# Padding a rank-one bias in attention scores from 64 to 128 partitions, in a two-layer decoder trunk

## The chip, the cores and the metric

The program runs on one core of a Trainium2 chip. The time is the device time of one execution in microseconds, and lower is better. A kernel's time is the median of several executions; the profile and the trace come from one execution of their own.

## The reference

The trunk has two layers over x of 256 tokens by 2048 channels, all in float32. Layer 0 mixes tokens by attention with a forget gate, layer 1 by a short gated convolution; each mixer is followed by an MLP of width 8192. Every sub-layer is normalised (RMSNorm), shifted and scaled by a vector worked out from c, and added back through a gate. The part that matters here is the attention of layer 0, with 16 heads of 128 channels:

```python
def fox_attention(q, k, v, log_f):
    F = jnp.cumsum(log_f.astype(jnp.float32), axis=-1)
    def one_block(args):                                    # 128 queries
        blk, q_i, F_i = args
        s = jnp.einsum('bhqd,bhkd->bhqk', q_i, k).astype(jnp.float32) * scale
        s = s + F_i[..., :, None] - F[..., None, :]
        q_pos = blk * Q_BLOCK + jnp.arange(Q_BLOCK)
        s = jnp.where(k_pos[None, :] <= q_pos[:, None], s, -jnp.inf)
        p = jax.nn.softmax(s, axis=-1)
        return jnp.einsum('bhqk,bhkd->bhqd', p.astype(v.dtype), v)
```

log_f is the log sigmoid of 16 forget logits per token, so F has one row of 256 values for each head. The term -F[s] is the same for all queries of a head.

## The kernel before

**Weights.** All products run on TensorE (PE) in a split form: every float32 operand becomes a high part (rounded by ACT) and a low part (the remainder, by DVE), and each product is three matmuls, high by high, low by high, high by low. Weights stream from memory through `raw` (four quarters of a unit of 2048 rows by 512 columns, issued by SP, queue `raw_arrived`). ACT writes `w_hi` (L790), DVE writes `w_lo` (L1183), both in a ring of four slots, each slot a pair of 128-row chunks. A unit has eight pairs. A slot is freed when PE has used it (`split_used`), and a quarter of `raw` when DVE has split it, so that SP then asks for the same quarter of the next unit. `chan_pair` (L428 to L430) makes q and k with channels on partitions, 24 matmuls of 256 columns a pair; `tok_pair` (L441 to L443) makes v and the outputs with tokens on partitions, 12 matmuls of 512 columns a pair.

**Beside it** POOL issues loads of the conditioning weights (`ada_raw`, four tiles), and DVE accumulates them (L1195, L1198) between its splits; the steps per slot are written out in tables. PE sums the result with ones (`ada_sum`).

**Attention.** Four groups of four heads. In the stream of each group PE calls `scores(g)` after an early pair of a unit (the pair of index 2 of unit 3 for group 0, index 1 of the v unit for the others), `turn_probs(g)` after its last pair, and `mix_values(g)` after the pair of index 2 of the next q unit (one unit later for group 0). Between them DVE takes the maxima (L1404, L1406), ACT the exponentials (L949), DVE normalises (L1421).

**`scores`** is the only reader of the two tiles of the change. For each of four heads and two query blocks it issues five matmuls into one group: three for q times k (L637 to L639), one that adds -F (L640), one that adds the causal mask (L641, weights `ident_r`). For query block 0 the first four cover 128 keys, for block 1 they cover 256; L641 covers 128. L640 is the special one: its weights are one column of `sel`, repeated 128 times, and it multiplies the tile `nf`.

**`nf` and `sel`.** `log_f` holds 64 columns: the 16 heads at columns 0 to 15 and again at 32 to 47, with zeros between and behind. A matmul with a triangle of ones (`upto`, L577) turns them into 64 rows of sums in PSUM. ACT copies them negated into `nf` [64, 256] (L914, rounded), and DVE puts the remainder into rows 32 to 47 (L1330). Column h of `sel` [64, 16] has ones in row h and row 32 + h, so that the matmul over 64 partitions picks the high and the low part of head h and adds them. Both tiles are filled or prepared by POOL at the start: memsets (L382 to L388), then the selections (L391 to L402), each raising `const_ready`. PE waits on it before its first transposition (L500, of the conditioning vector c by `ident`) and before the sums (L575), DVE before it copies the gates (L1322).

Of the kernel before, what the change touches and what calls it, by code (L numbers as in the profile page):

```python
# [5 lines left out]
F32 = mybir.dt.float32  # L6
F32R = mybir.dt.float32r
ACT = mybir.ActivationFunctionType
# [3 lines left out]
P = 128  # L12
D = 2048
T = 256
H = 16
# [10 lines left out]
NB = NU // P  # L26
# [76 lines left out]
def build(nc, x, c, ada_w, ada_b, norm_mix, norm_mlp, fox_w_in, fox_b_f, fox_w_out,  # L103
          conv_w_in, conv_w, conv_w_out, mlp_w_up, mlp_w_down, final_norm, out):
    ctx = ExitStack()
    with ctx:
        def sb(name, shape, dt=F32):
            return ctx.enter_context(nc.sbuf_tensor(name, shape, dt))

        def sem(name):  # L110
            return ctx.enter_context(nc.semaphore(name))

        def over(tensors):
# [6 lines left out]
            ("start_ring", [P, RING, 2, 2, NU], F32), ("xnT", [P, KC, T], F32), ("vrow", [VROWS, 4, P], F32),  # L120
            ("upto", [P, TT, T], F32), ("wf", [P, KC, H], F32), ("wf_hi", [P, KC, H], F32R), ("wf_lo", [P, KC, H], F32R)])
        _, conv_b, conv_c, _, gate = over([
            ("at_qs", [P, 2, QK, NU], F32), ("conv_b", [P, NB, T], F32), ("conv_c", [P, TT, NU], F32),
            ("to_vs", [P, QK, NU], F32), ("gate", [P, D], F32)])
# [6 lines left out]

        final_row, y = over([("final_row", [P, D], F32), ("y", [P, TT, D], F32)])
        _, square_out = over([("at_h", [P, 2 * (KC - 2) * T], F32), ("square_out", [P, 2 * NU], F32)])
        h = sb("h", [P, KC, 2, T], F32R)
        hb = sb("hb", [P, 2, EK, T])
# [24 lines left out]
        ident_r = sb("ident_r", [P, P], F32R)  # L160
        causal = sb("causal", [P, P], F32R)
        ones = sb("ones", [P, P])
        sel = sb("sel", [4 * H, H], F32R)
        vcol = sb("vcol", [P, 4, VROWS])
        c_col = sb("c_col", [P, KC])
        ca = sb("ca", [P, KC])
# [2 lines left out]
        gain = sb("gain", [P, KC])  # L169
        bf = sb("bf", [H, 1])  # L170
        log_f = sb("log_f", [P, TT, 4 * H])
        nf = sb("nf", [4 * H, T], F32R)
        f_tok = sb("f_tok", [P, TT, H])
        row_max = sb("row_max", [P, TT, NB])
        exp_bias = sb("exp_bias", [P, TT, NB])
# [10 lines left out]
        ps = ctx.enter_context(nc.psum_tensor("ps", [P, 8, NU], F32))  # L186
# [17 lines left out]
        const_ready = sem("const_ready")  # L204
# [34 lines left out]
        f_act = sem("f_act")  # L239
# [67 lines left out]
        def ada_tile(i, k):  # L307
            b, n = ADA[i]
            layer, part = PARTS[b]
            return ada_w[layer][P * k:P * (k + 1), D * part + NA * n:D * part + NA * (n + 1)]  # L310
# [69 lines left out]
        @block.gpsimd  # L380
        def _(pool):
            pool.memset(ident[:, :], 0.0).then_inc(const_ready, 1)  # L382
            pool.memset(ident_r[:, :].bitcast(F32), 0.0).then_inc(const_ready, 1)
            pool.memset(causal[:, :].bitcast(F32), 0.0).then_inc(const_ready, 1)
            pool.memset(upto[:, :, :], 1.0).then_inc(const_ready, 1)
            pool.memset(ones[:, :], 1.0).then_inc(const_ready, 1)
            pool.memset(sel[:, :].bitcast(F32), 0.0).then_inc(const_ready, 1)
            pool.memset(log_f[:, :, :], 0.0).then_inc(const_ready, 1)  # L388
            pool.wait_ge(const_ready, 7)
            for m in (ident, ident_r):  # L390
                pool.affine_select(out=m[:, :], in_=m[:, :].bitcast(F32), compare_op=ALU.not_equal, fill=1.0,  # L391
                                   base=0, pattern=[[-1, P]], channel_multiplier=1).then_inc(const_ready, 1)

            for i in range(2):
                pool.wait_ge(const_ready, 9 + i)
                pool.affine_select(out=sel[:, :], in_=sel[:, :].bitcast(F32), compare_op=ALU.not_equal, fill=1.0,
                                   base=-2 * H * i, pattern=[[-1, H]], channel_multiplier=1).then_inc(const_ready, 1)
            pool.affine_select(out=causal[:, :], in_=causal[:, :].bitcast(F32), compare_op=ALU.is_ge, fill=MASKED,
                               base=0, pattern=[[-1, P]], channel_multiplier=1).then_inc(const_ready, 1)
            for a in range(TT):  # L400
                pool.affine_select(out=upto[:, a, :], in_=upto[:, a, :], compare_op=ALU.is_ge, fill=0.0,
                                   base=-P * a, pattern=[[1, T]], channel_multiplier=-1).then_inc(const_ready, 1)  # L402

            for t in range(KC * A_END):
                if t < TILES:
                    pool.wait_ge(start_steps, START_STEPS[START_TILES - 1 + t // 2])
                    if t >= 2:
                        pool.wait_ge(start_used, START_TILES // 2)
                else:
                    pool.wait_ge(ada_steps, t - TILES + 1)  # L410
                pool.dma_start(ada_raw[:, t % TILES, :], ada_tile(t // KC, t % KC)).then_inc(ada_arrived[t % TILES], 16)  # L411

        @block.tensor
        def _(pe):
# [82 lines left out]
                return hooks  # L497


            pe.wait_ge(const_ready, 8)  # L500
            pe.wait_ge(c_arrived, 16)
            turn(ps[:, 4, 0:KC], vrow[0:KC, 0, :], ident[0:KC, 0:KC]).then_inc(c_turned, 1)
            pe.wait_ge(c_step, 4)
# [68 lines left out]

            def forget_sums():
                pe.wait_ge(f_step, 5)
                pe.wait_ge(const_ready, 14)  # L575
                for a in range(TT):
                    mm(ps[0:4 * H, 7, 0:T], log_f[:, a, :], upto[:, a, :], start=(a == 0), stop=(a == TT - 1))  # L577
                for b in range(TT):
                    for a in range(TT):
                        last = mm(ps[:, 7, T + H * b:T + H * (b + 1)], upto[:, a, P * b:P * (b + 1)], log_f[:, a, 0:H],  # L580
                                  start=(a == 0), stop=(a == TT - 1))
                last.then_inc(f_done, 1)
# [30 lines left out]
            for i in range(6):  # L613
                start_pair(n + i)
                if i == 2:
                    forget_turn()
                if i == 4:
                    forget_sums()
# [5 lines left out]
            def scores(g):  # L624
                pe.wait_ge(evacuated[(3 * g) % 2], (3 * g) // 2 + 1)
                pe.wait_ge(evacuated[(3 * g + 1) % 2], (3 * g + 1) // 2 + 1)
                pe.wait_ge(attn_ready, g)
                if g == 0:
                    pe.wait_ge(evacuated[0], 2)
                    pe.wait_ge(f_rows, 2)  # L630
                q = qs if g else mid[:, NB:2 * NB, :, :]
                for j in range(NB):
                    pick = sel[:, NB * g + j:NB * g + j + 1].broadcast_to([4 * H, P])
                    for b, o in ((0, ps[:, 6, P * j:P * (j + 1)]), (1, ps[:, 4 + j // 2, T * (j % 2):T * (j % 2 + 1)])):
                        n = P * (b + 1)
                        qh, ql = q[:, j, 0, P * b:P * (b + 1)], q[:, j, 1, P * b:P * (b + 1)]
                        mm(o, qh, ks[:, j, 0, 0:n], start=True, stop=False)  # L637
                        mm(o, qh, ks[:, j, 1, 0:n], start=False, stop=False)
                        mm(o, ql, ks[:, j, 0, 0:n], start=False, stop=False)  # L639
                        mm(o, pick, nf[:, 0:n], start=False, stop=False)  # L640
                        last = mm(o[:, n - P:n], ident_r[:, :], causal[:, :], start=False, stop=True)  # L641
                last.then_inc(scores_done, 1)
# [26 lines left out]
            for u in range(3, 3 * NG):  # L669
                g, t = u // 3, u % 3  # L670
# [87 lines left out]
            for i in range(3 * NG):  # L758
                g, t = i // 3, i % 3
# [21 lines left out]
        def _(act):  # L781
            op = nc.scalar.activation
# [128 lines left out]

            def forget_rows():
                act.wait_ge(f_done, 3)
                op(nf[:, :], ps[0:4 * H, 7, 0:T], ACT.Copy, scale=-1.0).then_inc(f_act, 1)  # L914

            def round_start(i):

# [20 lines left out]
            start_split(n + 8)  # L938
            start_split(n + 9)
            forget_rows()  # L940
            round_start(2)

# [30 lines left out]
            for u in range(3, 3 * NG):  # L973
                g, t = u // 3, u % 3
# [170 lines left out]
            for i in range(3 * NG):  # L1145
                g, t = i // 3, i % 3
# [29 lines left out]
        def _(dve):  # L1176
# [142 lines left out]

            def forget_copy():  # L1320
                dve.wait_ge(f_done, 2)
                dve.wait_ge(const_ready, 14)  # L1322
                for c0 in (0, 2 * H):
                    v.tensor_copy(log_f[:, :, c0:c0 + H], ps[:, 6, 64:64 + TT * H].rearrange("p (a h) -> p a h", a=TT)
                                  ).then_inc(f_step, 1)
# [61 lines left out]
            forget_log()  # L1387
            start_split(n + 4)
            forget_copy()
            start_split(n + 5)  # L1390
            low_start(0)
# [80 lines left out]
            for u in range(3, 3 * NG):  # L1472
                g, t = u // 3, u % 3
# [218 lines left out]
            for i in range(3 * NG):  # L1692
                g, t = i // 3, i % 3
# [40 lines left out]
```

## Time and profile before

| | us |
|---|---|
| median of three executions | 2396.4 |
| the three | 2382.73, 2396.4, 2397.29 |
| profiled execution, its own time | 2394.39 |
| its span, first to last instruction | 2392.7 |
| granted clock of TensorE over the span | 0.979 |

| engine | busy us | share of the span |
|---|---|---|
| PE matmuls | 2320.2 | 97% |
| PE weight loads | 1952.3 | 82% |
| DVE | 1630.4 | 68% |
| ACT | 1052.2 | 44% |
| POOL | 173.1 | 7% |

Matmuls overlap in the records: the duration of one is its latency, and the pace of the stream is read from the distance of the starts. PEld stands for the weight loads, which may run ahead of their matmul. The granted clock is a share of 2.4 GHz, so 0.50 is 1.2 GHz. The stage of q, k, v and attention lies between about 130 and 450 us; the output projection, MLP, convolution and second MLP follow. Calls of `scores` start at 164.52, 221.80, 310.56 and 395.95 us.

### The profile page before, as it was taken

What the parts mean: (1) busy time and instruction counts of PE and PEld (TensorE: products, weight loads), DVE (VectorE), ACT (ScalarE), POOL (GpSimd) and SP (SyncE); (2) the same over time, 40 slices, a digit from 0 to 9 for tenths busy, and PEclk for the clock granted to TensorE, in tenths of its full rate; (3) what the DMA queues carried; (4) which work ended last, traced back from release to release, by engine and by line L of the source; (5) the groups of instructions that cost most, each with busy time, mean ns of one, the idle gap of its engine ahead of it and who ended that gap; (6) DMA issues with size and microseconds to landing.
All of it is one profiled execution on the core that took longest, in us unless ns stands there. A gap on an engine that the chain in (4) does not pass through costs nothing.

```text
span 2392.7 us, 29047 instructions
## 1 busy us (share of the span) xinstructions
PE 2320.2 (97%) x11331; PEld 1952.3 (82%) x11331; DVE 1630.4 (68%) x1539; ACT 1052.2 (44%) x1183; POOL 173.1 (7%) x338
## 2 busy tenths in 40 slices
PE   5999999989999999999998999998999999999998
PEld 5988989768888888888886888876888888888886
DVE  5757877767866766776776888755786455455455
ACT  4344433445434434434444444444543443443443
POOL 0001111100100100100100111100010000000000
PEclk8999999999999999999998999999999999999999
DMA  9978878767977977987984899854896655655563
GB/s 364 387 247 282 310 275 334 269 245 246 313 274 246 314 277 239 323 281 227 324 282 161 312 339 332 310 164 153 280 320 208 194 189 185 191 192 190 190 201 122
DMA packets 270530, 615.61 MB, mean 257 GB/s; under 512 B 14704, under 2 KB 15040, under 8 KB 269504
## 3 DMA queue, kind: packets, MB, share of 16 engines
q1 hardware_dynamic: 220480, 437.29, 53.9%
q0 software_dynamic: 46080, 167.79, 19.7%
q10 hardware_dynamic: 3840, 8.68, 1.0%
q8 instruction: 95, 1.56, 0.3%
q14 instruction: 35, 0.29, 0.0%
HBM read 611.62 MB, written 2.10 MB: 257 GB/s over the span
## 4 chain that ended last, share of the span: by engine, by line
PE 90%; DMA 3%; DVE 3%; ACT 2%; issue 1%; SPq 0%; ACTq 0%; DVEq 0%
PE ps L441 26%; PE ps L443 26%; PE ps L442 26%; DMA start_ring<-in_ada_w_dram 3%; PE ps L428 2%; PE ps L430 2%; PE ps L429 2%; PE ps L720 1%; PE ps L481 1%; PE ps L478 1%; ACT w_hi L790 1%; DVE acc L1198 1%; DVE w_lo L1183 1%; PE ps L640 0%; PE ps L641 0%
## 5 line engine op out<-in xcount | busy, mean ns | idle before, releaser
L1183 DVE TENSOR_TENSOR w_lo<-raw,w_hi 128x1024 fp32r<-128x1024 f32 x740 | 903.8, 1224 | 624.8 <-ACT w_hi L790 622.5
L790 ACT ACTIVATE w_hi<-raw 128x1024 fp32r<-128x1024 f32 x740 | 783.6, 1060 | 1149.1 <-PE ps L443 1060.7
L441 PE MATMUL ps<-w_hi,h 128*128 128x512 f32 x1536 | 610.1, 397 | 6.5 <-DVE h L1296 6.5
L443 PE MATMUL ps<-w_lo,h 128*128 128x512 f32 x1536 | 602.6, 392 | 0.0
L442 PE MATMUL ps<-w_hi,h 128*128 128x512 f32 x1536 | 602.2, 392 | 0.0
L441 PE MATMUL ps<-w_hi,mid 128*128 128x512 f32 x1280 | 503.7, 393 | 2.6 <-DVE mid L1689 2.6
L443 PE MATMUL ps<-w_lo,mid 128*128 128x512 f32 x1280 | 499.6, 390 | 0.0
L442 PE MATMUL ps<-w_hi,mid 128*128 128x512 f32 x1280 | 499.2, 390 | 0.0
L441 PEld LDWEIGHTS ps<-w_hi,h 128*128 128x128 f32 x1536 | 291.4, 190 | 69.0 <-issue 9.3
L443 PEld LDWEIGHTS ps<-w_lo,h 128*128 128x128 f32 x1536 | 291.0, 189 | 62.1
L442 PEld LDWEIGHTS ps<-w_hi,h 128*128 128x128 f32 x1536 | 291.7, 190 | 59.2 <-issue 0.5
L411 POOL DMA_DIRECT2D ada_raw<-in_ada_w_dram x320 | 169.7, 531 | 1621.2 <-DVE acc L1195 571.0
L441 PEld LDWEIGHTS ps<-w_hi,mid 128*128 128x128 f32 x1280 | 241.1, 188 | 53.9 <-issue 4.5
L442 PEld LDWEIGHTS ps<-w_hi,mid 128*128 128x128 f32 x1280 | 241.2, 188 | 50.8 <-issue 1.4
L443 PEld LDWEIGHTS ps<-w_lo,mid 128*128 128x128 f32 x1280 | 240.9, 188 | 50.9
L1198 DVE SCALAR_TENSOR_TENSOR acc<-ada_raw,ca,acc 128x1024 f32<-128x1024 f32 x150 | 191.9, 1280 | 1.7 <-DMA ada_raw<-in_ada_w_dram 0.8
L1198 DVE SCALAR_TENSOR_TENSOR hb<-ada_raw,ca,hb 128x1024 f32<-128x1024 f32 x150 | 191.9, 1279 | 1.5 <-DMA ada_raw<-in_ada_w_dram 1.0
L428 PE MATMUL ps<-h,w_hi 128*128 128x256 f32 x512 | 149.0, 291 | 0.0
L430 PE MATMUL ps<-h,w_lo 128*128 128x256 f32 x512 | 147.3, 288 | 0.0
L429 PE MATMUL ps<-h,w_hi 128*128 128x256 f32 x512 | 147.3, 288 | 0.0
L428 PEld LDWEIGHTS ps<-h,w_hi 128*128 128x128 f32 x512 | 100.9, 197 | 0.2
L429 PEld LDWEIGHTS ps<-h,w_hi 128*128 128x128 f32 x512 | 101.1, 197 | 0.0
(201 smaller groups left out, 1248.6 us busy)
## 6 DMA issues: line engine op xcount, KB each, us to landing
ada_raw<-in_ada_w_dram POOLq DMA_DIRECT2D x320, 512.0 KB, 6.3
raw<-in_mlp_w_up_dram SPq DMA_DIRECT2D x128, 1024.0 KB, 5.3
raw<-in_mlp_w_down_dram SPq DMA_DIRECT2D x128, 1024.0 KB, 6.4
raw<-in_fox_w_in_dram SPq DMA_DIRECT2D x48, 1024.0 KB, 9.2
raw<-in_conv_w_in_dram SPq DMA_DIRECT2D x48, 1024.0 KB, 7.2
start_ring<-in_ada_w_dram SPq DMA_DIRECT2D x64, 512.0 KB, 11.7
raw<-in_fox_w_out_dram SPq DMA_DIRECT2D x16, 1024.0 KB, 7.7
raw<-in_conv_w_out_dram SPq DMA_DIRECT2D x16, 1024.0 KB, 5.2
```

The source lines that it names most:

```text
L411: pool.dma_start(ada_raw[:, t % TILES, :], ada_tile(t // KC, t % KC)).then_inc(ada_arrived[t % TILES], 16)
L428: mm(o, hi[:, jc], xh, start=(k == 0 and j % 2 == 0), stop=False, skip_group_check=True)
L429: mm(o, hi[:, jc], xl, start=False, stop=False, skip_group_check=True)
L430: last = mm(o, lo[:, jc], xh, start=False, stop=(k == KC - 1), skip_group_check=True)
L441: mm(o, xh, hi, start=(k == 0), stop=False)
L442: mm(o, xl, hi, start=False, stop=False)
L443: last = mm(o, xh, lo, start=False, stop=(k == KC - 1))
L478: last = mm(ps[:, SUM - 1 + b, :], ones[:, :], accs[slot][:, NU * b:NU * (b + 1)], start=True, stop=True)
L481: last = mm(ps[:, SUM, j:j + 1], accs[slot][:, P * j:P * (j + 1)], ones[:, 0:1], start=True, stop=True)
L790: op(w_hi[:, e % WR], raw[:, e // 2, EK * (e % 2):EK * (e % 2 + 1)], ACT.Copy).then_inc(hi_ready, 1)
L1183: v.tensor_tensor(w_lo[:, e % WR], raw[:, e // 2, EK * (e % 2):EK * (e % 2 + 1)], w_hi[:, e % WR].bitcast(F32), ALU.subtract).then_inc(spl ...
L1198: v.scalar_tensor_tensor(slot, src, ca[:, col:col + 1], slot, ALU.mult, ALU.add).then_inc(steps, 1)
```

## The change

`sel` and `nf` get 128 partitions. POOL sets all of `nf` to zero at the start, one instruction more, and all counts of `const_ready` rise by one. The partitions 64 to 127 of both stay zero; ACT and DVE write the same rows as before. L640 contracts over 128 partitions, and ACT waits for POOL before it writes `nf`.

```diff
@@ -160,7 +160,7 @@
-        sel = sb("sel", [4 * H, H], F32R)
+        sel = sb("sel", [P, H], F32R)
@@ -169,7 +169,7 @@
-        nf = sb("nf", [4 * H, T], F32R)
+        nf = sb("nf", [P, T], F32R)
@@ -386,13 +386,14 @@
             pool.memset(log_f[:, :, :], 0.0).then_inc(const_ready, 1)
-            pool.wait_ge(const_ready, 7)
+            pool.memset(nf[:, :].bitcast(F32), 0.0).then_inc(const_ready, 1)
+            pool.wait_ge(const_ready, 8)
...
-                pool.wait_ge(const_ready, 9 + i)
+                pool.wait_ge(const_ready, 10 + i)
@@ -497,7 +498,7 @@
-            pe.wait_ge(const_ready, 8)
+            pe.wait_ge(const_ready, 9)
             pe.wait_ge(c_arrived, 16)
@@ -572,7 +573,7 @@
             def forget_sums():
                 pe.wait_ge(f_step, 5)
-                pe.wait_ge(const_ready, 14)
+                pe.wait_ge(const_ready, 15)
@@ -630,7 +631,7 @@
                 for j in range(NB):
-                    pick = sel[:, NB * g + j:NB * g + j + 1].broadcast_to([4 * H, P])
+                    pick = sel[:, NB * g + j:NB * g + j + 1].broadcast_to([P, P])
@@ -911,7 +912,8 @@
             def forget_rows():
                 act.wait_ge(f_done, 3)
-                op(nf[:, :], ps[0:4 * H, 7, 0:T], ACT.Copy, scale=-1.0).then_inc(f_act, 1)
+                act.wait_ge(const_ready, 15)
+                op(nf[0:4 * H, :], ps[0:4 * H, 7, 0:T], ACT.Copy, scale=-1.0).then_inc(f_act, 1)
@@ -1319,7 +1321,7 @@
                 dve.wait_ge(f_done, 2)
-                dve.wait_ge(const_ready, 14)
+                dve.wait_ge(const_ready, 15)
```

The one place where an instruction is added is on POOL, ahead of the identity that PE's first transposition needs. POOL's order from the memset of `sel` on, in the kernel before:

```order
L387 MEMSET sel 64x16
L388 MEMSET log_f 128x128
L391 ISA
L391 AFFINE_SELECT ident<-ident 128x128
L391 AFFINE_SELECT ident_r<-ident_r 128x128
```

and in the changed kernel, whose lines behind the memset are one higher:

```order
L387 MEMSET sel 128x16
L388 MEMSET log_f 128x128
L389 MEMSET nf 128x256
L392 ISA
L392 AFFINE_SELECT ident<-ident 128x128
L392 AFFINE_SELECT ident_r<-ident_r 128x128
```

The memset of `nf` now stands between that of `log_f` and the two selections that make the identities, and everything behind it on POOL comes one memset later. On PE, DVE and ACT the instructions and their order are the same as before.

## Rows read from the trace of the kernel before

**Rows 1.** The page, part 1: busy us, share of the span, instructions.

```profile
PE 2320.2 (97%) x11331; PEld 1952.3 (82%) x11331; DVE 1630.4 (68%) x1539; ACT 1052.2 (44%) x1183; POOL 173.1 (7%) x338
```

**Rows 2.** Waits of PE, 130 to 420 us: total us, times, longest.

```profile
PE ps L648 <- DVE scratch L1421: 2.7, 2, 1.4
```

**Rows 3.** Line 640: count, ns min/median/max, first and last start, forms.

```profile
L640 PE MATMUL ps<-nf,sel x32: 322/382/579, 164.9 to 404.8; 64*128 64x128 f32 x16, 64*128 64x256 f32 x16
```

**Rows 4.** Timeline of PE, one head in `scores`: start us, us, what.

```profile
166.29 0.28 PE L637 MATMUL ps<-ks,mid 128*128 128x128 f32 x1
...
166.51 0.27 PE L639 MATMUL ps<-ks,mid 128*128 128x128 f32 x1
166.72 0.32 PE L640 MATMUL ps<-nf,sel 64*128 64x128 f32 x1
166.97 0.33 PE L641 MATMUL ps<-causal,ident_r 128*128 128x128 f32 x1
167.13 0.33 PE L637 MATMUL ps<-ks,mid 128*128 128x256 f32 x1
...
168.10 0.28 PE L637 MATMUL ps<-ks,mid 128*128 128x128 f32 x1
```

**Rows 5.** Timeline of PE, first of `mix_values(0)` and the matmul behind its last.

```profile
199.19 0.28 PE L661 MATMUL ps<-mid,vs 128*128 128x256 f32 x1
...
201.90 0.34 PE L428 MATMUL ps<-h,w_hi 128*128 128x256 f32 x1
```

**Rows 6.** Timeline of the weight loads, same head as rows 4.

```profile
166.45 0.19 PEld L639 LDWEIGHTS ps<-ks,mid 128*128 128x128 f32 x1
166.72 0.18 PEld L640 LDWEIGHTS ps<-nf,sel 64*128 64x128 f32 x1
166.97 0.19 PEld L641 LDWEIGHTS ps<-causal,ident_r 128*128 128x128 f32 x1
```

**Rows 7.** Timeline of PE around the first and the second call of `scores`.

```profile
164.16 0.28 PE L428 MATMUL ps<-h,w_hi 128*128 128x256 f32 x1
...
164.52 0.22 PE L637 MATMUL ps<-ks,mid 128*128 128x128 f32 x1
...
172.17 0.52 PE L428 MATMUL ps<-h,w_hi 128*128 128x256 f32 x1
...
174.67 0.28 PE L428 MATMUL ps<-h,w_hi 128*128 128x256 f32 x1
...
221.12 0.39 PE L441 MATMUL ps<-w_hi,h 128*128 128x512 f32 x1
...
221.80 0.22 PE L637 MATMUL ps<-ks,qs 128*128 128x128 f32 x1
...
231.34 0.73 PE L441 MATMUL ps<-w_hi,h 128*128 128x512 f32 x1
...
236.26 1.84 PE L481 MATMUL ps<-ones,acc 128*128 128x1 f32 x16
```

**Rows 8.** Windows: length, PE busy (count), granted clock, DMA share, GB/s.

```profile
225.60:235.80 10.20, 10.20 (x31) 0.50 0.62 239
...
399.70:409.80 10.10, 10.10 (x30) 0.50 0.90 346
170.95:174.30 3.35, 3.35 (x15) 0.51 0.33 130
...
199.20:201.90 2.70, 2.70 (x27) 1.00 0.95 325
```

**Rows 9.** Timeline of the first 9 us: POOL's widest memset; DVE after its copy.

```profile
1.24 0.53 POOL L385 MEMSET upto<- 128x512 f32 x1
...
8.72 0.17 DVE L1260 TENSOR_SCALAR ce<-ce 128x16 f32<-128x16 f32 x1 [5.52 <-ACT ce L830]
```

**Rows 10.** DMA busy share in tenths, 40 slices of 394 to 416 us.

```profile
DMA  9999999999999999999999999841000000000008
```

**Rows 11.** Waits of DVE, 150 to 450 us: total us, times, longest.

```profile
DVE acc L1198 <- DMA ada_raw<-in_ada_w_dram: 0.8, 1, 0.8
```

## The prediction

> **What bounds the kernel now.** The page's first part comes first: PE's matmuls are busy 97% of the span [rows 1]. The waits of PE between 130 and 420 us, the stage that makes q, k and v and runs the attention, hold one line of 2.7 us [rows 2]; so in that stage PE's own stream sets the pace, and what lengthens that stream lengthens the kernel. Then PE's timeline inside `scores`, the only user of the two tiles. Line 640 runs 32 times, all of them on 64 partitions [rows 3]: four heads, two query blocks each, in four calls.
>
> In one head's ten matmuls [rows 4] the starts tell the price of the 64-row matmul. From L639 to L640 it takes 0.21 us, from L640 to L641 0.25 us and from L641 to the next L637 0.16 us. Between neighbours that both have 128 rows the step is 0.11 us (166.29 to 166.51 is two of them). The whole head takes 168.10 - 166.29 = 1.81 us. For comparison, `mix_values` issues 24 matmuls on 128 rows, half of them 128 and half 256 columns wide, in 201.90 - 199.19 = 2.71 us [rows 5], 0.113 us each, whichever the width. Ten at that pace are 1.13 us. The weight loads say why [rows 6]: the load of L639 starts at 166.45, ahead of its matmul (166.51), while the loads of L640 and L641 start at 166.72 and 166.97, the very starts of their matmuls. Around the 64-row matmul nothing is loaded in advance, on the way in and on the way out.
>
> The second thing to see is the clock. Four stretches show half of the granted clock, 1.2 in place of 2.4 GHz, one at each call of `scores` [rows 8]: 225.6 to 235.8 at the second, one of the same length at the third, 399.7 to 409.8 at the fourth (0.50 each), and 170.95 to 174.3 (0.51) at the first. Ahead of the first two the engine had issued the stalled stream of `scores` for 6.4 and 3.8 us (from 164.52 and 221.80 [rows 7]). In `mix_values`, of the same matrix sizes without the 64-row matmul, the granted clock stayed at 1.00 [rows 8].
>
> **The change part by part.** *One more memset and a longer wait on POOL.* `nf` is 128x256; the 128x512 memset of `upto` took 0.53 us [rows 9], so this one costs 0.27 to 0.53, say 0.3. It delays the identity and with it the first transposition, whose product DVE copies, and then DVE sits idle for 5.52 us until ACT's exponential [rows 9]. That idle time covers it: nothing, and 0.3 us if it were gone. The other waits on `const_ready` come up at 150 us and later, when POOL has long been done; `sel` grows in partitions only, as does what L640 reads. The wait added on ACT before `nf` is written has no one behind it for the same reason. Nothing.
>
> *The switch between 64 and 128 rows, at full clock.* Four heads at 1.81 are 7.24 us a call. Four at 1.13 are 4.52; after a 128-wide group some steps of 0.17 stand in the old rows (a 256-wide one follows), so I take 4.55. Saved: 2.69 a call, 10.8 in four.
>
> The Trainium skill ("TensorEngine Tiling (Array Packing)", Key Properties) says that changing the tiling mode drains TensorE; 64 rows of 128 is a mode of its own there, and the trace agrees with a drain in the three late steps. Against this change speaks "TensorE: Matmul & The Clock Gate" (Why this matters for your kernels): a matmul on 32 rows takes the time of one on 128, so widening by itself would give nothing. By the first the sum stands; by the second alone it would be zero. The trace bears out both, since L640's own load is no shorter or longer, and the loss is at the borders.
>
> *The clock, if it no longer falls.* Read from [rows 7], as start of `scores`, its end, and the start after the twelve matmuls that follow. First call: 172.17 - 164.52 = 7.65, then twelve of L428 to L430 in 2.50 where full clock gives 12 x 0.12 = 1.44. Second call: 231.34 - 221.80 = 9.54, then twelve of L441 to L443 in 236.26 - 231.34 = 4.92 where full clock gives 12 x 0.227 = 2.72 (three took 0.68 ahead of the call). The third and fourth repeat the second, with half clock for as long [rows 8]. Beyond 7.24 at full clock the loss is 0.41 + 1.06 = 1.47 in the first and 2.30 + 2.20 = 4.50 in each of three: 15.0 in all. I take it as won back whole, since the new stream is 4.55 us at the pace of `mix_values`, which kept its clock. The other end is that nothing of it comes back: a stream of 4.55 us is longer than the 2.71 that the trace shows unharmed.
>
> *Does the rest follow?* The queue behind `scores` on PE is the next weight pairs. ACT and DVE split weights only as PE frees slots, so in `scores` they stand idle and start again when the next pair is done: their work, the maxima, exponentials and the turn of the probabilities all hang on that pair and move ahead with it. What could be late next is the transfers. Around the fourth call the DMA engines are full until about 408 us, then idle until 415 [rows 10]; the call began at about 395.9 if the clock fell 3.8 us into it, as in the second. With the change the next pair would end at 395.9 + 4.55 + 2.72 = 403.2, some 5 us before the queue runs dry. In the whole stage only 0.8 us of DVE's time waited for a transfer [rows 11]. I count nothing for this and price it as a rival.
>
> **Sum.** 10.8 + 15.0 = 25.8 us off the profiled execution's 2394.4, so 2368.6. The median of the three runs, 2396.4, lies 2.0 above that execution; on its scale the forecast is 2370.6.
>
> **Rivals.**
> *The clock falls all the same.* It would take back the 15.0: gain 10.8, 2385.6. For it: all four calls lost it, and the new ones still run 4.55 us of narrow matmuls. Against: `mix_values` did not.
> *The gain is eaten by transfers.* The stage keeps DMA full before each of the last three calls. If every slot needed its load at once, the restart would wait for the queue: 5 us at the fourth call, by the same reading at most as much at the second and third, none at the first, up to 15; with some 12, gain 14, 2382.6. Against: the 0.8 us above, and that the raw tiles are asked for a whole unit ahead.
> *It does not do what it says.* If the late loads came from the data (one column repeated 128 times as weights) and not from the rows, the steps stay: 2396.4. Against: L641 has plain weights and is late too. The skill's rule on few rows, above, would by itself land here too.
> *Slower.* The same cause, but with twice the rows to fetch the stall doubles: 0.68 more for each of 16 heads, 10.8 more, 2407.2. It needs the load's time to grow with its rows, and decides from any growth above zero; 128-row loads take 0.19 us where L640's takes 0.18 [rows 6], so nearly nothing speaks for it.
>
> **How the numbers follow.** Forecast 0.78, clock falls 0.08, transfers 0.09, no effect 0.04, slower 0.01. The forecast's own spread comes from the other stretches of half clock in the program, which can fall longer or shorter (one like those above is worth 4.5), and from the runs of before, which lie 14.6 us apart: 2362 to 2380 (two such stretches below the forecast, two above). To hold 8 in 10 I reach up through the two partial gains to 2386. About 1% (24 us) is what a measurement can tell from no change, and the limit for faster by over 1% is 2372.4, close above the forecast; a little over six tenths of its 0.78 lie beyond it, 0.48. Within 1%: 0.51. Slower by over 1%: 0.01, since even the slower rival stays within.
>
> **What would show it.** In the changed profile L640 has 128 rows, its weight load starts ahead of its matmul, all steps are 0.11 to 0.17, a call of `scores` takes 4.5 to 4.8 us, and the granted clock is 1.00 through each call and the pair behind it. DVE's idle time at each call shrinks by as much, and q/k/v and attention end about 26 us earlier. Wrong would be: steps of 0.2 and more at L640 or L641; half clock at `scores`; new waits of PE on w_lo or of DVE on transfers between 240 and 450 us.

## The result and the profile after

The changed kernel took 2370.02 us (median of six executions, 2369.65 to 2373.3), the kernel before 2389.26 us (six, 2382.73 to 2397.29). The ratio is 0.9917, 95% interval 0.9896 to 0.9939: faster by 0.8%. The forecast was 2370.6; it had set out from a median of 2396.4, which more executions of before brought down.

The head and part 1 of the page of the changed kernel, which answer to [rows 1]:

```profile
span 2368.4 us, 29049 instructions
PE 2302.1 (97%) x11331; PEld 1944.2 (82%) x11331; DVE 1629.6 (69%) x1539; ACT 1052.0 (44%) x1183; POOL 172.6 (7%) x339
```

The span is 24.3 us shorter with the same number of matmuls. Lines behind the memset stand one higher, so L641 is the bias matmul that was L640. Its record, to be read against [rows 3]:

```profile
L641 PEld LDWEIGHTS ps<-nf,sel x32: 187/190/193, 164.9 to 381.9; 128*128 128x128 f32 x32
L641 PE MATMUL ps<-nf,sel x32: 273/278/283, 165.0 to 382.0; 128*128 128x128 f32 x16, 128*128 128x256 f32 x16
```

It has 128 rows, its median latency fell from 382 to 278 ns, and the last call is over at 382.2 us where it was at 405.5. PE's timeline in the second call, which answers to [rows 4] and [rows 7] (start us, us, what):

```profile
217.84 0.22 PE L638 MATMUL ps<-ks,qs 128*128 128x128 f32 x1
217.89 0.28 PE L639 MATMUL ps<-ks,qs 128*128 128x128 f32 x1
218.01 0.27 PE L640 MATMUL ps<-ks,qs 128*128 128x128 f32 x1
218.12 0.27 PE L641 MATMUL ps<-nf,sel 128*128 128x128 f32 x1
218.23 0.27 PE L642 MATMUL ps<-causal,ident_r 128*128 128x128 f32 x1
218.34 0.34 PE L638 MATMUL ps<-ks,qs 128*128 128x256 f32 x1
...
222.34 0.45 PE L442 MATMUL ps<-w_hi,h 128*128 128x512 f32 x1
```

All steps into and out of L641 shown here are 0.11 us (0.11 to 0.12 in the rest of the call), and the call takes 222.34 - 217.84 = 4.50 us, where it took 9.54. The weight loads are in advance again, as the loads of L641 and L642 show against [rows 6]:

```profile
166.06 0.19 PEld L641 LDWEIGHTS ps<-nf,sel 128*128 128x128 f32 x1
166.17 0.19 PEld L642 LDWEIGHTS ps<-causal,ident_r 128*128 128x128 f32 x1
```

Their matmuls start at 166.12 and 166.23. The windows of the four calls (length, PE busy, PEld, DVE, ACT, POOL, granted clock, DMA share, GB/s) show a granted clock of 1.00, where [rows 8] had 0.50:

```profile
164.70:169.20 4.50, 4.50 (x42) 4.50 (x41) 3.24 (x3) 1.06 (x1) 0.96 (x2) 1.00 0.91 314
217.90:222.30 4.40, 4.40 (x41) 4.40 (x40) 3.50 (x3) 1.06 (x1) 0.98 (x2) 1.00 0.98 350
299.50:303.90 4.40, 4.40 (x41) 4.40 (x40) 3.95 (x4) 1.06 (x1) 0.80 (x3) 1.00 1.03 397
377.70:382.10 4.40, 4.40 (x40) 4.40 (x39) 4.40 (x5) 1.06 (x1) 0.53 (x1) 1.00 1.02 391
```

### The profile page after: what moved, and what is told of

Its sections match the earlier page's. It is cut to its first block, busy times and chain, and to the rows that moved or that the text cites. A ratio compares the mean times of both kernels' runs of the same rounds, so it can differ in the third digit from the quotient of the medians.

```text
span 2368.4 us, 29049 instructions
## 1 busy us (share of the span) xinstructions
PE 2302.1 (97%) x11331; PEld 1944.2 (82%) x11331; DVE 1629.6 (69%) x1539; ACT 1052.0 (44%) x1183; POOL 172.6 (7%) x339
## 4 chain that ended last, share of the span: by engine, by line
PE 90%; DVE 3%; DMA 3%; ACT 2%; issue 1%; SPq 0%; ACTq 0%; DVEq 0%
PE ps L442 26%; PE ps L444 26%; PE ps L443 26%; DMA start_ring<-in_ada_w_dram 3%; PE ps L429 2%; PE ps L431 2%; PE ps L430 2%; PE ps L721 1%; PE ps L482 1%; PE ps L479 1%; ACT w_hi L791 1%; DVE acc L1200 1%; DVE w_lo L1185 1%; PE ps L516 1%; ACT scratch L951 0%
## 6 DMA issues: line engine op xcount, KB each, us to landing
start_ring<-in_ada_w_dram SPq DMA_DIRECT2D x64, 512.0 KB, 11.7
```

## The experiments

Each run is timed beside the kernel before on the same chip. The ratio given with its 95% interval need not be the quotient of the two medians beside it. Three questions: is it the border between row counts, or something else in the change or in the matmul; which row counts have a border; and what does the half clock hang on.

### The tiles alone

```diff
-    pick = sel[:, NB * g + j:NB * g + j + 1].broadcast_to([P, P])
+    pick = sel[0:4 * H, NB * g + j:NB * g + j + 1].broadcast_to([4 * H, P])
...
-    mm(o, pick, nf[:, 0:n], start=False, stop=False)
+    mm(o, pick, nf[0:4 * H, 0:n], start=False, stop=False)
```

> The changed kernel, with L641 reading only partitions 0 to 63 of the two larger tiles: the added memset and waits stay, the width of the matmul goes back. Theory (the borders between 64 and 128 rows cost the time): one head takes 1.81 us again, the calls 7.6 to 9.6 us, half clock of 3.4 to 10.2 us at each call, and the time is that of the kernel before, within 3 us. Rival (larger tiles or the order of the start do it): the time of the changed kernel, 2370.

Measured: 2389.04 us against 2390.32 of before, ratio 0.9999 (0.9986 to 1.0013). The profile has the stalls and the half clock back; windows of this kernel, with the same columns as above:

```profile
170.60:177.40 6.80, 6.80 (x25) 5.67 (x26) 0.00 (x0) 0.00 (x0) 0.21 (x1) 0.50 0.49 179
228.60:238.80 10.20, 10.20 (x31) 7.97 (x31) 0.04 (x1) 0.00 (x0) 0.53 (x1) 0.50 0.67 259
317.40:327.60 10.20, 10.20 (x31) 7.97 (x31) 0.31 (x1) 0.00 (x0) 0.53 (x1) 0.50 0.68 259
402.70:412.90 10.20, 10.20 (x31) 7.96 (x32) 2.88 (x3) 0.00 (x0) 1.05 (x2) 0.50 0.91 343
```

So the memset, the waits and the larger tiles do nothing that shows; the gain comes with the rows that the matmul reads.

### 96 and 48 rows

The changed kernel with `sel[0:6 * H, ...]` and `nf[0:6 * H, 0:n]`, and the kernel before with `sel[0:3 * H, ...]` and `nf[0:3 * H, 0:n]`.

> The changed kernel, with L641 reading partitions 0 to 95. Theory in its first form (any count of rows other than 128 stalls the stream at its borders): as before, 2389, with steps of 0.21 and 0.25 us around L641. Theory in its second form (the array is set either to 64 rows or to the whole, and 96 needs the whole): no stall, calls of 4.5 us, 2370.

Measured: 2369.33 us against 2390.32, ratio 0.9913 (0.9897 to 0.993). Its four calls take 4.55 to 4.57 us at a granted clock of 1.00. Of the two forms of the theory the second fits. The line in its profile:

```profile
L641 PE MATMUL ps<-nf,sel x32: 273/276/285, 165.6 to 382.7; 96*128 96x128 f32 x16, 96*128 96x256 f32 x16
```

> The kernel before, with L640 reading only partitions 0 to 47, all that it needs. Theory (the array is set to 64 rows for anything up to 64 that is more than 32, and each border costs 0.34 us): as before, heads of 1.81 us, half clock at all calls, 2390. Rival (the stall grows with the rows, which would also let 96 of 128 look free by chance): heads shorter than 1.81, time below 2386.

Measured: 2392.32 us against 2389.99, ratio 1.0003 (0.9991 to 1.0015). From this profile, the line and the clock at the first two calls:

```profile
L640 PE MATMUL ps<-nf,sel x32: 322/380/579, 164.9 to 405.1; 48*128 48x128 f32 x16, 48*128 48x256 f32 x16
```

```profile
170.80:177.60 6.80, 6.80 (x30) 6.35 (x30) 0.00 (x0) 0.00 (x0) 0.00 (x0) 0.50 0.19 71
228.80:235.60 6.80, 6.80 (x20) 5.28 (x20) 0.00 (x0) 0.00 (x0) 0.00 (x0) 0.50 0.67 256
```

At the third and fourth call the half clock lasts 10.2 us each, as before. Forty-eight rows stall like 64 (median 380 and 382 ns) and 96 run like 128 (276 and 278). The stall does not grow with the rows; the step lies between 64 and 96. Counts of 32 and less, and those between 64 and 96, were not run.

### 64 rows with fewer borders

Two orders of the same matmuls on 64 rows. In the first the eight bias matmuls of a call open it (`start` set once for each bank, the first writer):

```diff
+    for b in range(TT):
+        for j in range(NB):
+            pick = sel[:, NB * g + j:NB * g + j + 1].broadcast_to([4 * H, P])
+            mm(out(b, j), pick, nf[:, 0:P * (b + 1)], start=(j == 0 or (b == 1 and j == 2)), stop=False,
+               skip_group_check=True)
     for j in range(NB):
         for b in range(TT):
...
-            mm(o, pick, nf[:, 0:n], start=False, stop=False)
```

> The kernel before with its 64 rows, but the eight matmuls of L640 of a call stand together at its front: one border in and one out in place of eight each. Theory (the border costs, not the 64-row matmul): 8 borders in and out cost 2.7 us a call, so one costs 0.34; calls of 4.9 us, no half clock at them, 2372. Rival (the 64-row matmul with one repeated column of weights is itself slow, 0.2 us and more each): eight of them still cost 2 us or more, calls of about 7 us and most of the time of before, 2385.

Measured: 2370.81 us against 2390.32, ratio 0.9915 (0.9898 to 0.9932). PE's timeline of the first call:

```profile
165.31 0.28 PE L430 MATMUL ps<-h,w_lo 128*128 128x256 f32 x1
165.52 1.18 PE L638 MATMUL ps<-nf,sel 64*128 64x128 f32 x8
166.62 0.33 PE L644 MATMUL ps<-ks,mid 128*128 128x128 f32 x1
166.79 0.28 PE L645 MATMUL ps<-ks,mid 128*128 128x128 f32 x1
...
170.32 0.33 PE L428 MATMUL ps<-h,w_hi 128*128 128x256 f32 x1
```

It takes 0.21 us to enter; then the eight 64-row matmuls and the way out take 1.10 us. Between the eight the steps are 0.11 to 0.17 us, the step out is 0.20. A 64-row matmul among its like is as cheap as one on 128 rows, repeated column of weights or not, and the rival with the slow data is out. The granted clock is 1.00 through all four calls.

In the second order the two bias matmuls of each head stand together, ahead of the head's other eight.

> The kernel before with its 64 rows, but the two matmuls of L640 of a head stand together: four borders in and out a call in place of eight. Theory: half the stall, 1.3 us of 2.7, is left; calls of 5.9 us at full clock, 5.4 us over all less than before from this alone. What it tells of the clock: if half clock comes with any stall, 3.4 to 10.2 us of it remain at the calls and the time is about 2380; if it needs the stream as thin as before, none remains and the time is about 2375.

Measured: 2374.95 us against 2390.32, ratio 0.9934 (0.9918 to 0.9951). PE's timeline around its first call, and the windows of its four calls:

```profile
165.03 0.28 PE L430 MATMUL ps<-h,w_lo 128*128 128x256 f32 x1
165.24 0.49 PE L636 MATMUL ps<-nf,sel 64*128 64x128 f32 x2
...
171.06 0.33 PE L428 MATMUL ps<-h,w_hi 128*128 128x256 f32 x1
```

```profile
165.30:171.00 5.70, 5.70 (x40) 4.96 (x40) 3.10 (x3) 1.06 (x1) 1.05 (x2) 1.00 0.91 321
219.80:225.50 5.70, 5.70 (x40) 4.96 (x40) 3.43 (x3) 1.06 (x1) 1.05 (x2) 1.00 1.02 377
302.80:308.60 5.80, 5.80 (x41) 5.05 (x41) 3.91 (x4) 1.06 (x1) 1.13 (x3) 1.00 1.03 392
382.50:388.20 5.70, 5.70 (x40) 4.95 (x40) 5.09 (x5) 1.06 (x1) 1.37 (x3) 1.00 1.03 397
```

Both orders open a call with 64 rows, so the first way in lies ahead of its first matmul. The fair measure is therefore from the start of the last matmul ahead of the call to the start of the first behind it. For the changed kernel the first call gives 169.24 - 164.57 = 4.67 us:

```profile
164.57 0.28 PE L431 MATMUL ps<-h,w_lo 128*128 128x256 f32 x1
164.69 0.23 PE L638 MATMUL ps<-ks,mid 128*128 128x128 f32 x1
...
169.24 0.33 PE L429 MATMUL ps<-h,w_hi 128*128 128x256 f32 x1
```

The first call in four kernels, by the number of excursions to 64 rows in it (each has a border in and one out):

| excursions a call | kernel | call alone, us | with the step into it, us | over none, for each excursion |
|---|---|---|---|---|
| 0 | changed | 4.55 | 4.67 | |
| 1 | bias matmuls first | 4.80 | 5.01 | 0.34 |
| 4 | paired | 5.82 | 6.03 | 0.34 |
| 8 | before, at full clock (4 x 1.81) | 7.24 | 7.36 | 0.34 |

The cost is in proportion to the excursions. In the other three calls, behind matmuls of 512 columns, the single excursion costs 0.39 us and the paired ones 0.35 each. The times roughly follow: 1.36 + 3 x 1.40 = 5.6 us for the paired kernel over the changed one, against 4.9 between the medians 2374.95 and 2370.02, which come from different sets of executions.

### What the half clock hangs on

The pairs have half the stall and kept the clock whole. Two more runs ask whether length or density decides. First the changed kernel with each call issued twice:

```diff
-                for j in range(NB):
+                for j in 2 * list(range(NB)):
```

> The changed kernel, with the matmuls of each call of scores issued twice over, the second pass overwriting the first with the same values; all on 128 rows. It asks whether the half clock of before came from the length of the narrow stream or from its stalls. Theory (the stalls): calls of 9.0 us, longer than 7.24 of before, keep the full clock, and the time is 4 x 4.5 = 18 us over the changed kernel, 2388. Rival (any narrow stream of this length loses the clock): half clock of 3.4 to 10.2 us at the calls and some 10 to 15 us more, 2400.

Measured: 2388.51 us against 2389.99, ratio 0.9993 (0.998 to 1.0006): 18.3 us over the changed kernel. Windows that lie in its last three calls:

```profile
224.20:233.20 9.00, 9.00 (x81) 9.00 (x80) 3.55 (x3) 1.06 (x1) 1.05 (x2) 1.00 1.00 370
310.40:319.40 9.00, 9.00 (x81) 9.00 (x80) 3.97 (x4) 1.06 (x1) 1.19 (x3) 1.00 1.03 400
393.20:402.20 9.00, 9.00 (x81) 9.00 (x80) 5.07 (x5) 1.06 (x1) 1.58 (x3) 1.00 1.03 396
```

Then the same doubling of the paired kernel on 64 rows:

> The kernel of the pairs (64 rows, the two bias matmuls of a head together, calls of 5.8 us, no half clock), with each call's matmuls issued twice over. It asks whether the pairs kept the clock because their calls are short or because their stream is denser. If it is the length of the stalled stream: calls of 11.6 us or more fall to half clock, and the time is 2375 + 4 x 5.8 = 2398 plus 5 to 20. If it is the density: full clock through 11.6 us, and 2398.

Measured: 2398.27 us against 2389.38, ratio 1.0037 (1.0022 to 1.0053). Its calls take 11.74 us each. The windows of the last three:

```profile
226.40:238.10 11.70, 11.70 (x81) 10.13 (x81) 3.45 (x3) 1.06 (x1) 1.05 (x2) 1.00 0.88 336
315.40:327.00 11.60, 11.60 (x80) 10.03 (x80) 3.85 (x4) 1.06 (x1) 1.07 (x3) 1.00 0.89 340
400.90:412.60 11.70, 11.70 (x81) 10.12 (x81) 5.31 (x5) 1.06 (x1) 1.58 (x3) 1.00 1.03 396
```

A stream with half of the stalls keeps the full clock through 11.7 us, longer than the 9.5 of before; with all of them the clock falls 6.4 us into the first call and 3.8 us into each of the others [rows 7, rows 8]. So the clock did not fall for how long the stream lasted, nor for any stall as such, but with how closely the stalls stood, that is with how thin the stream was. The number of borders and the thinness go together in these runs and are not told apart.

### A further step, and the changed kernel again

The last experiment asks whether on 128 rows the weight loads set the pace of this stream, 0.113 us a matmul. The eight mask matmuls of a call have the same weights and the same values, so three wide ones of 512, 256 and 256 columns can do their work, with five loads fewer (`masked(n)` is the mask repeated n times):

```diff
+    mm(ps[:, 6, :].rearrange("p (j t) -> p j t", t=P), ident_r[:, :], masked(NB), start=True, stop=False,
+       skip_group_check=True)
+    for i in range(2):
+        mm(ps[:, 4 + i, :].rearrange("p (j t) -> p j t", t=T)[:, :, P:T], ident_r[:, :], masked(2), start=True,
+           stop=False, skip_group_check=True)
...
-    last = mm(o[:, n - P:n], ident_r[:, :], causal[:, :], start=False, stop=True)
```

> The changed kernel with the eight mask matmuls of a call (128 columns each) put together as three at its front, of 512, 256 and 256 columns; the bias matmul closes each group. If in this stream each weight load costs 0.113 us whatever the width up to 256, five loads fewer save 0.57 and the 512-wide one adds some 0.1: 0.4 to 0.5 us a call, calls of 4.05 us, 1.8 us over all: 2368.2 against 2370.0. If the pace is not set by the loads, calls stay at 4.5 us and the time does not move.

> The changed kernel once more, on the chip of these runs, for comparison with them: 2370, its runs within 1 us of each other where those of before lie 15 us apart, since before loses between 3.4 and 10.2 us at half clock at each call and this kernel none.

Measured: the merged masks 2367.46 us (four executions, 2367.06 to 2368.39), the changed kernel 2370.17 (four, 2369.62 to 2370.46), before 2389.99 (19, 2381.99 to 2396.43). Against before, the ratios are 0.9896 (0.988 to 0.9913) and 0.9907 (0.9891 to 0.9924). The merged version is the fastest here: its slowest execution is faster than the fastest of the changed kernel. Its opening in the second call:

```profile
218.89 0.39 PE L636 MATMUL ps<-causal,ident_r 128*128 128x512 f32 x1
219.11 0.40 PE L639 MATMUL ps<-causal,ident_r 128*128 128x256 f32 x2
219.35 0.22 PE L646 MATMUL ps<-ks,qs 128*128 128x128 f32 x1
...
223.02 0.40 PE L442 MATMUL ps<-w_hi,h 128*128 128x512 f32 x1
```

A call takes 4.13 us in place of 4.50, so fewer loads do save time, 0.37 us of the 0.4 to 0.5 expected. Over four calls this makes 1.5 of the 2.7 us between the medians, and the twelve matmuls behind each call are 0.2 us shorter in all. Where the other 1.0 comes from is open.

## Why the prediction was right, point by point

**The bound.** PE's stream set the pace and still does. By the calls and the twelve matmuls behind each, the profiled execution before spent 53.5 us [rows 7], with the third and fourth like the second; the changed kernel spent 27.9 (4.55 + 1.48, then three times 4.50 + 2.80). That is 25.6 us, and the spans differ by 24.3.

**The switch.** Forecast 2.69 us a call, measured 7.24 - 4.50 = 2.74. Both the size and the cause stand: the tiles alone changed nothing, and the cost went with the number of borders, 0.34 us an excursion. The runs agree with the rule of the Trainium skill ("TensorEngine Tiling (Array Packing)", Key Properties) that a change of tiling mode drains TensorE, though no record shows the drain itself. The rule that the prediction set against the change, from the Trainium skill's "TensorE: Matmul & The Clock Gate" (Why this matters for your kernels), that a matmul on 32 rows takes the time of one on 128, has its like here only among matmuls of one kind: steps of 0.11 to 0.17 us between eight on 64 rows. No run had 32 rows.

**The clock.** Forecast: it no longer falls at any call. It fell at none in the profiled execution, as the windows show, nor in that of the same kernel profiled again, and the run with doubled calls leaves much room. On the profiled execution of before the term was sized right: 15.0 forecast, and 25.6 - 4 x 2.74 = 14.6 measured.

**The measured saving is smaller than the sum**, 19.2 us between the medians and not 25.8, and the term that was mis-sized is this one, as a mean over executions. How long the half clock lasts changes from one execution to the next: 3.4, then three times 10.2 us in the one profiled before [rows 8], 6.8 and three times 10.2 with the tiles alone, 6.8 twice and 10.2 twice with 48 rows. The granted clocks of whole executions say the same: of the 44 executions of before in the three later sets, the two fastest, 2380.96 and 2381.09 us, had 0.988, and the eight above 2394 us had 0.978 to 0.982. The fastest stand where the borders alone would put them, 2370.17 + 11.0 = 2381.2. These are means over the whole execution and do not say where in it the clock fell. Nineteen executions of before have a median of 2389.99, so against 2370.17 the two terms together are 19.8 us; 4 x 2.74 = 11.0 are the borders, and some 9 are left for the clock where 15 were counted.

The forecast took its profiled execution for typical, and the three executions then at hand (two of them at 2396 and 2397) seemed to bear it out. That the forecast time held in spite of this is because the changed kernel has nothing at the calls that varies: its profiled execution, 2370.1, and its median agree, and most of the error sits in the base that was subtracted from. How closely it held, 2370.6 against 2370.02, is luck as well. The sum on the profiled execution alone gave 2368.6, and the profiled execution of the changed kernel took 2370.1, 1.5 us more. The 2.0 us added to pass from the profiled execution to the median had the wrong sign, since with more executions the median of before (2389.26, 2389.99) lies over 4 us below the profiled one (2394.39); the two errors nearly cancel.

**What followed behind.** The transfers took nothing that shows, though DVE's waits for them rose; in the changed kernel, between 130 and 430 us (total us, times, longest):

```profile
DVE acc L1200 <- DMA ada_raw<-in_ada_w_dram: 2.0, 2, 1.5
```

DVE waited 2.0 us where it was 0.8 [rows 11]. That is off the path: PE's own waits in this stage are the same as before. A window of 130 to 420 us seems to say otherwise, 3.9 us in three places for the normalised probabilities against 2.7 in two [rows 2]. But the stage now ends earlier, and the third wait of before lies behind that window's end. First before, then the changed kernel:

```profile
425.43 0.33 PE L648 MATMUL ps<-ident,scratch 128*128 128x128 f32 x1 [1.23 <-DVE scratch L1421]
```

```profile
399.95 0.33 PE L649 MATMUL ps<-ident,scratch 128*128 128x128 f32 x1 [1.21 <-DVE scratch L1423]
```

With the window drawn behind it, both kernels wait 3.9 us in three places. DVE's idle time at the calls did shrink, as forecast: its longest wait for ACT's `w_hi` in this stage fell from 12.1 to 5.0 us.

**From 25.6 to 24.3.** Set matmul against matmul in the two traces, the changed kernel enters the first call 0.2 us late and is 25.5 us ahead at 520 us of before's time. It is 24.4 us ahead at 544 us. Between them PE's clock stands at half, around the start of the first MLP, where PE is idle for much of the time, and in the changed kernel it stays there longer (columns as in the windows above; first before, then the changed kernel):

```profile
529.40:539.60 10.20, 4.48 (x12) 3.46 (x13) 7.00 (x15) 5.71 (x10) 0.00 (x0) 0.50 0.33 103
```

```profile
502.90:516.60 13.70, 6.96 (x20) 5.33 (x21) 9.01 (x17) 5.71 (x10) 0.00 (x0) 0.50 0.29 86
```

Two later stretches of this kind, 13.7 us before and 10.2 now, then 10.2 and 13.7, give 0.9 us and take it back. The prediction had these stretches in its range and not in its sum. Why they fall longer or shorter is open.

**The start.** The memset of `nf` took 0.32 us, forecast 0.3:

```profile
2.04 0.32 POOL L389 MEMSET nf<- 128x256 f32 x1
...
8.78 0.17 DVE L1262 TENSOR_SCALAR ce<-ce 128x16 f32<-128x16 f32 x1 [5.36 <-ACT ce L831]
```

DVE's idle time behind its copy went from 5.52 [rows 9] to 5.36, so it was covered, as said.

**The rivals.** That the clock falls all the same: no half clock at any call. Transfers: above. That the late loads come from the data: refuted by the order with the bias matmuls first. Slower: the loads take 0.19 us with 128 rows. By the bound of 1% the outcome, 0.8%, is within 1%, the side that had 0.51.

## What to carry to other kernels

A matmul whose contraction has 48 or 64 rows, alone among full ones, costs its stream 0.34 us beyond the time that it takes among its like; fill it up with zeros (96 and 128 rows cost nothing here), or gather such matmuls so that they share one excursion. The page shows PE as busy throughout; the steps between starts, the loads that no longer run ahead and the granted clock beside such a stream give the stall away. Before a saving is subtracted from one profiled execution, see whether what is saved varies between executions.

## What the runs showed of the hardware that was not expected

In the four counts of rows that were run the loss is there in full or not at all (48 and 64 rows against 96 and 128), and it is linear in the excursions: 0.34 us for each at the first call with one, four and eight of them, at 2.4 GHz. The clock followed the stalls and not the length: the stream with eight excursions a call went to 1.2 GHz in every profile taken of it, the one with four stayed at 2.4 GHz even when doubled to 11.7 us. And the time itself varied more in the kernels that lost the clock: 14 to 18 us between executions of before in one set, 11.3 with the tiles alone, though only 5.5 with 48 rows, against 0.8 to 4.4 us for the kernels that kept the clock at the calls.
